# One block with one weight stream for the z projection, the SSD output projection and the long convolution

## What is computed

```
z  = p[..., COL_Z:COL_XBC]
yz = (y * silu(z)).reshape(bsz, L, 4, 512)          # gated_rmsnorm, four groups
yz = yz * lax.rsqrt(mean(yz * yz, axis=-1) + EPS);  y_ssd = yz.reshape(bsz, L, 2048) * g
kf = hyena_filters(L, lp)                           # sin MLP, decay, / sum|k|, rfft
u3 = short_conv(p[..., COL_HY:COL_GATE], ...);      v, x1, x2 = split(u3, 3)
z2 = x1 * fft_long_conv(v, kf[:, 0], hy_bias[0])
y_hy = x2 * fft_long_conv(z2, kf[:, 1], hy_bias[1])
gates = sigmoid(p[..., COL_GATE:] + gate_b)
merged = gates[..., :D] * (y_ssd @ w_ssd_out) + gates[..., D:] * (y_hy @ w_hy_out)
```

## Time and profile before

| | |
|---|---|
| time before, median of 3 runs | 2642.38 us (2639.52 to 2642.42) |
| profiled execution, its own time | 2643.38 us |
| its span | 2641.6 us |
| TensorE busy in the span | 2334.3 us (88%) |
| VectorE, ScalarE, GpSimd busy | 1520.1, 1032.1, 203.6 us |
| mean granted TensorE clock | 0.931 of full speed |
| z stage, first to last matmul | 654.84 to 791.95 us |
| SSD output stage | 798.79 to 908.37 us |
| Hyena stage | 921.71 to 1531.46 us |

### The profile page before, as it was taken

How to read it: one execution, slowest core, us unless ns; L and a number is a source line. 1 busy time by engine, 2 the same in 40 slices (tenths; PEclk the granted TensorE clock), 3 DMA queues, 4 the chain that set the end, 5 groups by cost and what they waited for, 6 DMA issues and landing times. The chain is left out here.

```text
span 2641.6 us, 34797 instructions
## 1 busy us (share of the span) xinstructions
PE 2334.3 (88%) x12901; PEld 1886.5 (71%) x12901; DVE 1520.1 (58%) x1934; ACT 1032.1 (39%) x1278; POOL 203.6 (8%) x145
## 2 busy tenths in 40 slices
PE   6699988997768798888888999987799999999995
PEld 1288877454658797777777899965588888878773
DVE  1345552565434255767675544453655568989986
ACT  1423321111433242323233333332234446777773
POOL 1000000000000003333333100000000000000000
PEclk9899995998888999999999999998699999999998
DMA  9733320998434553333333456562156668999993
GB/s 370 286 113 93 94 83 22 360 347 308 141 95 155 166 162 100 116 101 116 111 118 105 122 163 183 183 248 59 64 192 191 191 209 320 382 351 365 375 336 129
DMA packets 285401, 503.49 MB, mean 191 GB/s; under 512 B 18757, under 2 KB 158576, under 8 KB 283494
## 3 DMA queue, kind: packets, MB, share of 16 engines
q1 hardware_dynamic: 280310, 481.54, 54.3%
q0 software_dynamic: 4976, 20.43, 2.2%
HBM read 499.78 MB, written 2.13 MB: 190 GB/s over the span
## 5 line engine op out<-in xcount | busy, mean ns | idle before, releaser
L189 DVE TENSOR_TENSOR w_lo<-raw,w_hi 128x1024 fp32r<-128x1024 f32 x720 | 917.8, 1287 | 670.4 <-ACT w_hi L185 643.8
L185 ACT ACTIVATE w_hi<-raw 128x1024 fp32r<-128x1024 f32 x720 | 760.9, 1060 | 842.5 <-PE bank L197 824.4
L195 PE MATMUL bank<-h_hi,w_hi 128*128 128x256 f32 (+1 forms) x1664 | 514.4, 309 | 42.4 <-DVE w_lo L189 29.0
L197 PE MATMUL bank<-h_hi,w_lo 128*128 128x256 f32 (+1 forms) x1664 | 508.1, 305 | 0.0
L196 PE MATMUL bank<-h_lo,w_hi 128*128 128x256 f32 (+1 forms) x1664 | 508.1, 305 | 0.0
L195 PEld LDWEIGHTS bank<-h_hi,w_hi 128*128 128x128 f32 x1664 | 321.0, 193 | 60.0 <-issue 29.5
L196 PEld LDWEIGHTS bank<-h_lo,w_hi 128*128 128x128 f32 x1664 | 320.8, 193 | 14.3 <-issue 1.9
L197 PEld LDWEIGHTS bank<-h_hi,w_lo 128*128 128x128 f32 x1664 | 320.7, 193 | 12.8
L195 PE MATMUL bank<-w_hi,ys_hi 128*128 128x512 f32 x384 | 154.2, 402 | 17.8 <-DVE p_tmp L1855 11.4
L263 PE MATMUL bank<-raw,cpad 128*32 128x512 f32 x768 | 148.9, 671 | 20.5 <-DMA raw<-in_ada_w 20.3
L195 PE MATMUL bank<-ys_hi,w_hi 128*128 128x256 f32 x512 | 148.3, 290 | 17.4 <-ACT merged L1347 10.6
(11 more groups left out here) (358 smaller groups left out, 3103.6 us busy)
## 6 DMA issues: line engine op xcount, KB each, us to landing
raw<-in_w_in SPq DMA_DIRECT2D x240, 512.0 KB, 3.8
raw<-in_ada_w SPq DMA_DIRECT2D x192, 512.0 KB, 7.6
raw<-in_moe_w_gate SPq DMA_DIRECT2D x128, 512.0 KB, 6.0
raw<-in_moe_w_up SPq DMA_DIRECT2D x128, 512.0 KB, 6.0
raw<-in_moe_w_down SPq DMA_DIRECT2D x128, 512.0 KB, 5.9
raw<-in_w_ssd_out SPq DMA_DIRECT2D x32, 512.0 KB, 3.4
raw<-in_w_hy_out SPq DMA_DIRECT2D x32, 512.0 KB, 3.4
raw<-in_w_o SPq DMA_DIRECT2D x32, 512.0 KB, 3.6
```

The source lines that it names most:

```text
L185: act.activation(self.k.w_hi[:, j % HL, :], self.k.raw[:, j % RAW, :], ACT.Copy).then_inc(self.hi_ready, 1)
L189: dve.tensor_tensor(self.k.w_lo[:, j % HL, :], self.k.raw[:, j % RAW, :], self.k.w_hi[:, j % HL, :].bitcast(F32), ALU.subtract).then_inc(s ...
L195: pe.matmul(out, lhs[0], rhs[0], start=start, stop=False)
L197: return pe.matmul(out, lhs[1], rhs[0], start=False, stop=stop)
```

## The change

The three stages become one block with one stream of 192 slabs, without loops: 32 of z, 4 of a gate block, 32 of the SSD output, 96 of the Hyena projections, and 28 of the other seven gate blocks (before: 32, 32, 96 and 32). The number of slabs, matmuls and bytes stays the same.

- The z rounds take turns on banks 0, 1 and 4, 5, so that `z_round(i)` waits for the gate of round i-2.
- The first gate block stands behind the last z round. It is kept in `merged`, and `first_out` (VectorE) multiplies the first SSD output block into it.
- The turn of the last group stands behind the third slab of the SSD output, whose first slabs are ordered so that they need that group late (`out_step`).
- The SSD output takes turns on banks 4, 5 and 6, 7; `keep` stands in ScalarE's queue in the middle of a block.
- POOL loads the tables and the first filter when the last z group is split.
- `bias` and the butterfly become `taps` on VectorE. `load_filter` on POOL waits for it.

The core of the diff:

```
-                    pe.wait_ge(s.gate, i + 1)                       # z project(i)
+                def z_round(i):
+                    if i >= 2:
+                        pe.wait_ge(z.gate, i - 1)
...
+                                mm = mm3(pe, k.psum[4 * (i % 2) + t][:], ...
...
+                z_round(0)
+                for i in range(1, GROUPS):
+                    z_round(i)
+                    z_turn(i - 1)
+                pe.wait_ge(z.gate, GROUPS - 1)
+                for q in range(4):
+                    quarter(GATE0 + q, q, 0, (k.h_hi[:, 0], k.h_lo[:, 0]))
+                for n in range(32):
+                    out_slab(n)
+                    if n == 2:
+                        z_turn(GROUPS - 1)
+                pe.wait_ge(z.sig, 1)
                 pe.wait_ge(s.tables, 48)
...
+                for n in range(HY0):                                 # ScalarE
+                    st.split_hi(act, 0, 192, n)
+                    i = n // 8
+                    if n <= 38:
+                        if 2 <= i and n % 8 == 1:
+                            z_highs(i - 2)
+                        if i and n % 8 == 3:
+                            gate(i - 1)
+                        if i and n % 8 == 4:
+                            squares(i - 1)
+                        if i and n % 8 == 5:
+                            root(i - 1)
+                    if n == 39:
+                        first_gate()
+                    if n == 41:
+                        z_highs(GROUPS - 1)
+                    if n >= 46 and n % 4 == 2:
+                        keep((n - 42) // 4)
...
+                for n in range(HY0):                                 # VectorE
+                    st.split_lo(dve, 0, 192, n)
+                    i = n // 8
+                    if n <= 38:
+                        if 2 <= i and n % 8 == 1:
+                            z_lows(i - 2)
+                        if i and n % 8 == 3:
+                            gated(i - 1)
+                        if i and n % 8 == 5:
+                            norm(i - 1)
+                    if n == 41:
+                        z_lows(GROUPS - 1)
+                    if n == 45:
+                        first_out()
...
-                def bias(n):
+                def taps(n):
...
-                    dve.tensor_tensor(hs[0:1, 0, :], hs[0:1, 0, :], brow[:], ALU.add).then_inc(s.bias, 1)
+                    own.own(dve, dve.tensor_tensor(hs[0:1, 0, :], hs[0:1, 0, :], brow[:], ALU.add))
+                    own.inc(dve.tensor_tensor(ktab[:, 0:2, :], hs[:, 0::2, :], hs[:, 1::2, :], ALU.add))
+                    own.own(dve, dve.tensor_tensor(ktab[:, 2:4, :], hs[:, 0::2, :], hs[:, 1::2, :], ALU.subtract))
+                    dve.tensor_tensor(hs[:, 0::3, :], ktab[:, 0::2, :], ktab[:, 1::2, :], ALU.add)
+                    dve.tensor_tensor(hs[:, 1:3, :], ktab[:, 0::2, :], ktab[:, 1::2, :], ALU.subtract).then_inc(s.bfly, 1)
```

More of the change, by code:

```diff
@@ L1066, in build @@
         nrm = place("p4_nrm", [P, 8], at=after("p4_full"))
[L1067 to L1071, removed]
+        k.merged = place("merged", [P, KT, L], at=cl)
+        z = Box()
+        (z.gate, z.yz, z.sq, z.ms, z.root, z.scaled, z.turned, z.full, z.hi, z.lo, z.sig, z.kept, z.kept0) = sems(
+            "p4", "gate", "yz", "sq", "ms", "root", "scaled", "turned", "full", "hi", "lo", "sig", "kept", "kept0")
         def gate_out_src(half, w_out):
@@ L1081, in build @@
         w_ssd = wview(io["w_ssd_out"][0])
-        def ssd_out_src(i, j):
-            return w_ssd[:, 4 * (j % 4):4 * (j % 4) + 4, ds(i * 512 + (j // 4) * 256, 256)]
-        hyo_src = gate_out_src(1, wview(io["w_hy_out"][0]))
[L1088 to L1097, removed]
-                    pe.wait_ge(s.gate, i + 1)
[L1099 to L1215, removed]
@@ L1216, in build, with gate_src, ssd_out_src, hy_src @@
-        st.done += 32
-        st.base += 32
-        k.merged = place("merged", [P, KT, L], at=cl)
+        def gate_src(g, q):
+            return w_in[:, 4 * q:4 * q + 4, ds(g * 256 + COL_GATE, 256)]
+        def ssd_out_src(b, q):
+            return w_ssd[:, 4 * q:4 * q + 4, b * 256:(b + 1) * 256]
+        def hy_src(j):
+            i, part, b = j // 24, j % 24 // 8, j % 8
+            return w_in[:, 4 * (b % 4):4 * (b % 4) + 4, ds(i * 512 + COL_HY + part * D + (b // 4) * 256, 256)]
+        GATE0, OUT0, HY0, GATE1 = 32, 36, 68, 164
@@ L1399, in build @@
         LEAD = (CONV - HY_SHORT) // 2
-        NB = 32
+        NB = 31
         def lanes(i):
-            return 6 if i < 4 else 8
+            return 6 if i < 4 else 7
         with nc.Block() as block:
@@ L1463, in _ @@
                     if i:
-                        butterfly(2 * i - 2)
                         load_filter(2 * i - 1)
@@ L1469, in _ @@
                             load_decay(i)
-                        butterfly(2 * i - 1)
                     if i < 4:
@@ L1574, in _, with gate, squares @@
             def _(act):
+                def gate(i):
+                    act.wait_ge(st.w_used, 8 * i + 8 + HL + st.base)
+                    if i:
+                        act.wait_ge(z.turned, i)
+                    for t in range(TT):
+                        ins = act.activation(gz[:, t, :], k.psum[4 * (i % 2) + t][:], ACT.Silu)
+                    ins.then_inc(z.gate, 1)
+                def squares(i):
+                    act.wait_ge(z.yz, i + 1)
+                    for t in range(TT):
+                        if t == 1:
+                            act.wait_ge(z.sq, i * 2 + 1)
+                        act.activation(sq[:], gz[:, t, :], ACT.Square, accum_out=nrm[:, t:t + 1]).then_inc(z.sq, 1)
@@ new lines, in root, with z_highs, first_gate @@
+                def root(i):
+                    act.wait_ge(z.ms, i + 1)
+                    act.activation(nrm[:, 4:6], nrm[:, 2:4], ACT.Sqrt).then_inc(z.root, 1)
+                def z_highs(i):
+                    act.wait_ge(z.full, i + 1)
+                    act.activation(k.ys_hi[:, 4 * i:4 * i + 4, :], full4[:], ACT.Copy).then_inc(z.hi, 1)
+                def first_gate():
+                    act.wait_ge(st.w_used, GATE0 + 4 + HL + st.base)
+                    for c in range(2):
+                        bias = VEC_AT["gate_b"] + c
+                        ins = act.activation(k.merged[:, c, :], k.psum[c][:, 0:L], ACT.Sigmoid,
+                                             bias=k.vcol[:, bias:bias + 1])
+                    ins.then_inc(z.sig, 1)
@@ new lines, in keep @@
+                def keep(b):
+                    act.wait_ge(st.w_used, OUT0 + (8 if b == 1 else 4 * b + 4) + HL + st.base)
+                    for c in range(2):
+                        ins = act.activation(k.merged[:, 2 * b + c, :], k.psum[4 + 2 * (b % 2) + c][:, 0:L], ACT.Copy)
+                    ins.then_inc(z.kept, 1)
+                for n in range(HY0):
[16 more added lines that the diff above has]
+                        keep((n - 42) // 4)
@@ L1644, in _, with gated, norm @@
                 own = k.own
+                def gated(i):
+                    dve.wait_ge(z.gate, i + 1)
+                    dve.tensor_tensor(gz[:], gz[:], k.y[:, :, i * GC:(i + 1) * GC], ALU.mult).then_inc(z.yz, 1)
+                def norm(i):
+                    dve.wait_ge(z.sq, i * 2 + 2)
+                    dve.tensor_scalar(nrm[:, 2:4], nrm[:, 0:2], 1.0 / GC, EPS, ALU.mult, ALU.add).then_inc(z.ms, 1)
+                    dve.wait_ge(z.root, i + 1)
+                    own.own(dve, dve.reciprocal(nrm[:, 6:8], nrm[:, 4:6]))
+                    for t in range(TT):
+                        ins = dve.tensor_scalar(gz[:, t, :], gz[:, t, :], nrm[:, 6 + t:7 + t], None, ALU.mult)
+                    ins.then_inc(z.scaled, 1)
@@ L1769, in _ @@
                         if i and pp == 0:
-                            bias(first)
+                            taps(first)
                         if i and pp == 1:
@@ L1776, in _ @@
                         if i and pp == 3:
-                            bias(second)
+                            taps(second)
                         if i and pp == 4:
                             product(second)
-                merge(7)
-        st.done += 128
-        st.base += 128
+                merge(6)
+        st.done += 192
+        st.base += 192
         w_o = wview(io["w_o"][0])
```

164 lines of the change are left out of this document (87 added, 77 removed).

## The result

The changed kernel takes 2507.8 us (median of 4 runs, 2505.3 to 2509.7) against 2642.4 us. The ratio is 0.9488 with a 95% interval of 0.9471 to 0.9505: 5.1% faster. The forecast was 2506. The profiled execution took 2508.5 us, its span is 2507.0 us; before they were 2643.4 and 2641.6 us.

A forecast was written before the change was run, and what follows sets the result against it. TensorE, 88% busy, sets the time and idles in these stages only for reasons of order. Savings of 79.5 + 42.2 + 13.4 + 2.0 = 137.1 us from 2643.4 give 2506.3, median about 2506; likeliest case 2496 to 2518, range 2494 to 2540.

The forecast's parts named there:

- Joined block up to the Hyena projections: z rounds, gate block and SSD output rebuilt from full-clock pieces: 198.9 us, so projections begin 68.0 us earlier.
- late slab: Rival, 14%: turns and gates stop TensorE in four places of the joined block; 8 to 32 us come back, 2514 to 2538.
- the last group's chain and the two seams: TensorE idle before the Hyena projections: 10.9 us for Silu, squares, root and scale; seams of 6.8 and 13.34 us.
- The wait for the butterfly: Hyena stage: TensorE's eight waits for POOL's last step, 42.2 us, all go with four VectorE operations taking 5.1 us.
- The spectra at half clock: Eight stretches from spectrum to forward transform, 53.8 us, shrink to 5.0 us each: 13.4 us saved, bounds 0 and 18.
- The first five projections: Start of the Hyena projections: without the seam in front, 57.6 + 0.2 us in place of 59.85, 2.0 us saved.
- the sum: All savings together: 79.5 + 42.2 + 13.4 + 2.0 = 137.1 us.
- the clock should stay at 2.4 GHz: Spectra in the Hyena stage: without the stop before them TensorE keeps full clock, part of the 13.4 us saved.
- The forecast's last step: From profiled execution to median: 2643.4 - 137.1 = 2506.3, and a median of about 2506 us.
- VectorE's new work is off the path: Against the rival, 13%, that TensorE waits for `taps` in place of POOL: 2520, or 2562 us.
- The rival with the clock as its mechanism: Slower, 2%: TensorE's clock swings throughout the joined block; with 375 us at half clock, 2678 us.
- the sum without any further cost of the switch: ScalarE's chain behind a z turn: table loads of 1.28 us without drains; drains would add about 5 us in total.

The follow-up runs named there:

- experiment 6: Changed kernel with the four scalings of each z group done twice on VectorE: 2512.2 us, ratio 0.9502.
- experiment 3: Changed kernel with all z rounds in one bank pair (banks 0 and 1), each waiting for Silu of the round before: 2540.0 us, ratio 0.9601.
- experiment 5: Changed kernel with ScalarE's `keep` back behind the fourth split of the block after next, as in the kernel before: 2514.9 us, ratio 0.9518.
- experiment 1: Changed kernel with only the butterfly of the filters put back on POOL: 2562.7 us, ratio 0.969 to the kernel before.
- experiment 2: Kernel before, its three blocks kept, with the butterfly on VectorE as the only change: 2587.2 us, ratio 0.9779.
- experiment 10: The changed kernel itself run and profiled once more, nothing altered: 2508.8 us, ratio 0.949.
- experiment 4: Changed kernel with the first pair of butterfly operations done three times, four more VectorE operations per filter: 2521.2 us, ratio 0.9532.

## Why the prediction was right

By its steps, each against the profiled execution:

- *Joined block up to the Hyena projections*: 198.9 us forecast, 197.0 measured. So 69.9 us are gained against 68.0, and the gate block of 11.5 is moved as foreseen. No late slab: experiment 6 shows that the margin behind a turn was really as thin as 0.2 to 0.5 us, and experiments 3 and 5 that bank pairs and the place of `keep` are what removed the waits for Silu and `keep` (33.9 and 11.3 us of this stretch with the half clock behind them). The rest, some 25 us, belongs to the last group's chain and the two seams; no experiment takes these apart.
- *The wait for the butterfly*: 42.2 us forecast. All of it went, shown in both directions by experiments 1 and 2. Four operations took 4.8 us where 5.1 were reckoned; the slack at the fifth spectrum was 2.1 us against 1.8.
- *The spectra at half clock*: 13.4 us forecast, 53.75 - 41.19 = 12.6 measured. The start of the forward transform was put at 5.0 us behind the spectrum by ScalarE's queue, and stands at 5.10 (twice 5.29).
- *The first five projections*: 2.0 forecast, 59.85 - 57.69 = 2.2 measured.
- *What had no term*: 7.3 us were lost in the first profiled execution, by half clock at the first filter (1.0 us), at the four even turns (9.54 - 7.26 = 2.3 us, all eight counted) and in the four projections behind them (4.1 us). From the first z matmul to the end of the joined block it saves 876.6 - 744.3 = 132.3 us where the sum has 137.1. In experiment 10 it is 741.1 us, 135.5 saved, with 4.5 us lost behind odd filters; without either loss both would be at about 737. Of the steps, "the clock should stay at 2.4 GHz" held only in part: in the spectra it does, but it fell behind the filters. Why it falls behind a pause of 1.29 us at one filter and not at the next is not settled: one kernel shows both (experiment 10), so no comparison of single profiles can tell whether an order ends it. The kernel before has the same pauses and no such loss in its profile.
- *Luck in the total*: the profiled execution came out 2.2 us above its forecast of 2506.3, and the block alone 4.8. Some 2.5 us were gained outside the block, where nothing was changed (the first z matmul came 1.5 us earlier); that is less than the 8 us by which the first z matmul moves between two executions. The forecast's last step is also 1 us high by its own terms, since 137.1 from a median of 2642.4 is 2505.3.

The rivals: VectorE's new work is off the path, though not far (experiment 4: 4.9 us more a filter cost 13 us). Late slabs did not appear, and appear at once with 1.7 us more in the chain. The rival with the clock as its mechanism was nearest in kind, since what is missing in the sum is half clock, but it is 7 us and not 170: over 197 us with two bank pairs in turn the granted clock was 0.99. The Trainium skill ("TensorE: Matmul & The Clock Gate", A second HAM failure mode) tells of another kernel in which cycling through PSUM banks lets the engine idle briefly between its groups of matmuls, so that the clock swings. This trace shows neither over that stretch: TensorE was busy for all of the 197.00 us. In round 2 the table load begins at 705.22 us, behind a split that ends at 705.20, and Silu begins at 706.51, 1.29 us after the load, so the sum without any further cost of the switch was right. The Trainium skill ("ScalarE: Activation LUTs", What ACT_TABLE_LOAD costs) adds a drain of 1.38 us, which this trace does not show.

## What to carry to other kernels

When TensorE is the bound, rebuild the stretch from full-clock pieces and put every wait in the queue where its releaser is already done. Here one block, a second bank pair and moved waits together were worth 70 us, and the thinnest margin (0.2 to 0.5 us) can be found by adding up the chain behind the release. A serial helper chain in front of a matmul costs its wait and then the half-clock matmuls behind it, here 42 us and 13 us, so price both. A matmul that waits for its bank to be copied out can often be given independent matmuls to run meanwhile: mixing two groups that were already neighbours gave 14 us more.

## What the runs showed of the hardware

- VectorE is slower beside POOL's butterfly: a `split_lo` took up to 3.43 us in place of 1.23. With the butterfly on VectorE the longest of all 720 takes 2.32 us, and their mean fell from 1287 to 1237 ns; with the butterfly back on POOL (experiment 1) the mean is 1287 and the longest 3.42 again. That gain was in no term, and what it was worth in time no run separates.
- The clock can fall within a stretch in which TensorE never pauses for more than 1.29 us, behind the filter matmuls (over 64 partitions), with or without transposes next to them, and where it falls differs from one execution to the next. Of the changed kernel's two profiles one has it at all four even filters (three of them at 1031, 1147 and 1263 us) and at no odd one, the other at three odd ones (1093, 1209, 1325 us) and at no even one. Each such even filter cost 1.5 to 2.7 us, each odd one 1.5.
- Single stops of 1.2 to 1.8 us within dense projections (experiments 5 and 6) cost at most 0.5 us more than themselves on average (11.3 us for 8.8, 4.9 for 4.1); longer ones cost 1.7 us more each in the filters (13.5 us for eight, experiment 1) and 2.2 in the z rounds (9 us for four, experiment 3).
